# Whose engine makes the low halves of the key matrices: GpSimd instead of VectorE in the slab stage, with five gathered rows per slab instead of three

## What is computed

```python
def peer_ffn(h, w_q, sub_keys, u_tab, v_tab):
    tok = h.reshape(b * L, d)
    q = (tok @ w_q).astype(jnp.float32).reshape(n, PEER_HEADS, 2, PEER_DKEY // 2)
    s1 = jnp.einsum('nhk,ek->nhe', q[:, :, 0], sk[0])
    s2 = jnp.einsum('nhk,ek->nhe', q[:, :, 1], sk[1])
    ...
    gate = jax.nn.softmax(top_s, axis=-1)
    def run_block(args):
        t, g, e = args
        act = jax.nn.gelu(jnp.einsum('nd,nhkd->nhk', t, u_tab[e]), approximate=False)
        return jnp.einsum('nhk,nhkd->nd', g * act, v_tab[e])
```

## Time and profile before

| | us |
|---|---|
| runs of the kernel before (3) | 2326.02, 2326.99, 2332.55 |
| median | 2326.99 |
| profiled execution, its own time | 2322.12 |
| span of the profile in it | 2320.3 |
| slab stage (from the trace) | 1356 to 1608 |
| tail | 1608 to 1660 |
| value stage | 1665 to 2286 |

### The profile page before, as it was taken

The page is one execution under the profiler, slowest core; times in us unless marked ns, Lnnn a source line. Parts: engine busy times, 40 slices in busy tenths (PEclk is TensorE's granted clock), DMA queues, the critical chain, the costliest instruction groups (busy, mean ns, idle before and its releaser), DMA issues.

```text
span 2320.3 us, 34474 instructions
## 1 busy us (share of the span) xinstructions
PE 2108.4 (91%) x12253; PEld 1755.1 (76%) x12253; DVE 1546.9 (67%) x3300; ACT 745.0 (32%) x1111; POOL 814.7 (35%) x498
## 2 busy tenths in 40 slices
PE   7988899998979997999999989999898899898983
PEld 7988895555643347999999989999777777677772
DVE  1155314555572331179779889998888889898898
ACT  2122113443430002134434346654323232333231
POOL 2322330000210003346776641112644355565550
PEclk9998999999988998999999999999999999999997
DMA  9999996875968674235666667788999999999992
GB/s 356 356 357 345 345 356 272 337 310 195 311 243 302 232 282 133 65 108 170 216 222 222 211 229 285 278 300 344 388 394 394 393 393 393 385 394 377 394 393 89
DMA packets 200422, 682.89 MB, mean 294 GB/s; under 512 B 18432, under 2 KB 84352, under 8 KB 194304
## 3 DMA queue, kind: packets, MB, share of 16 engines
q1 hardware_dynamic: 151696, 508.36, 61.1%
q0 software_dynamic: 46080, 167.79, 19.1%
q10 hardware_dynamic: 2544, 5.48, 0.6%
HBM read 618.78 MB, written 196.32 MB: 351 GB/s over the span
## 4 chain that ended last, share of the span: by engine, by line
PE 33%; issue 23%; DMA 22%; DVE 15%; POOL 4%; ACT 3%; SPq 0%; ACTq 0%; DVEq 0%; POOLq 0%
DMA overlay<-peer_v 16%; PE bank L188 7%; PE bank L189 7%; PE bank L190 7%; DMA overlay<-peer_u 3%; DVE overlay L2142 3%; DVE arena L1964 2%; POOL overlay L1535 2%; PE bank L1951 2%; DVE arena L1959 2%; POOL overlay L340 2%; PE bank L601 2%; PE bank L585 2%; PE bank L651 1%; PE bank L624 1%
## 5 line engine op out<-in xcount | busy, mean ns | idle before, releaser
L188 PE MATMUL bank<-overlay 128*128 128x384 f32 (+4 forms) x2856 | 983.6, 344 | 110.6 <-DVE overlay L2146 64.4
L189 PE MATMUL bank<-overlay 128*128 128x384 f32 (+4 forms) x2856 | 967.2, 339 | 0.0
L190 PE MATMUL bank<-overlay 128*128 128x384 f32 (+4 forms) x2856 | 966.1, 338 | 0.0
L188 PEld LDWEIGHTS bank<-overlay 128*128 128x128 f32 x2856 | 556.3, 195 | 164.5 <-issue 85.6
L189 PEld LDWEIGHTS bank<-overlay 128*128 128x128 f32 x2856 | 556.2, 195 | 30.6
L190 PEld LDWEIGHTS bank<-overlay 128*128 128x128 f32 x2856 | 554.9, 194 | 32.3
L1535 POOL TENSOR_TENSOR overlay<-overlay 128x1024 fp32r<-128x1024 f32 x98 | 253.7, 2594 | 196.5 <-ACT overlay L1527 196.3
L1794 POOL DMA_INDIRECT arena<-peer_v,arena x160 | 239.7, 1498 | 180.7 <-DVE arena L1964 165.1
L1794 POOL DMA_INDIRECT arena<-peer_rows,arena x136 | 161.4, 1187 | 327.4 <-DVE arena L1959 307.0
L1964 DVE SCALAR_TENSOR_TENSOR arena<-arena 128x1024 f32<-128x1024 f32 x160 | 204.5, 1278 | 0.1
L1527 ACT CAST overlay<-overlay 128x1024 fp32r<-128x1024 f32 x144 | 150.8, 1049 | 142.1 <-DMA overlay<-peer_u 137.3
(11 more groups left out here) (233 smaller groups left out, 2073.9 us busy)
## 6 DMA issues: line engine op xcount, KB each, us to landing
overlay<-peer_u SPq DMA_DIRECT2D x128, 512.0 KB
overlay<-peer_v SPq DMA_DIRECT2D x128, 512.0 KB
o_ks<-cache_k SPq DMA_DIRECT2D x16, 4088.0 KB, 27.1
o_vsall<-cache_vall SPq DMA_DIRECT2D x16, 4088.0 KB, 37.5
arena<-cache_kT SPq DMA_DIRECT2D x32, 896.0 KB, 11.7
arena<-cache_v SPq DMA_DIRECT2D x56, 512.0 KB, 6.5
arena<-w_out SPq DMA_DIRECT2D x48, 512.0 KB, 5.8
act<-arena SPq DMA_DIRECT2D x128, 192.0 KB
```

The lines of the kernel that those rows point to most:

```text
L188: pe.matmul(out, lhs[0], rhs[0], start=start, stop=False)
L189: pe.matmul(out, lhs[0], rhs[1], start=False, stop=False)
L190: return pe.matmul(out, lhs[1], rhs[0], start=False, stop=stop)
```

## The change

- `ROW_TURNS` goes from (2, 5, 7) to (1, 2, 4, 5, 7): VectorE does five `dot`s per slab, 60 in the slab stage for 36. `DONE` goes from 60 to 84 with the tail's 24, and the rows left for the value stage from 236 to 212.
- VectorE's 46 low parts of rows 82 to 127 are gone (36 of them in the slabs, 10 in the tail); GpSimd makes them in `pool_gather`, between its gathers, with the same function as for the earlier rows. The count `u_lo2` is gone: TensorE and SyncE wait for `u_lo` throughout.
- The two gelus of row sums stand after three and after six groups of value matrices.

```diff
+        query_lo = []
...
+            query_lo.append(lo)
...
-        ROW_TURNS = (2, 5, 7)
+        ROW_TURNS = (1, 2, 4, 5, 7)
         SLAB_ROWS, TAIL_ROWS = SLABS * len(ROW_TURNS), (PK - TAIL) * 2
+        DONE_ROWS = SLAB_ROWS + TAIL_ROWS
...
-            for g in range(2 * UROWS - EARLY_ROWS):
+            def low(a):
+                if EARLY + LEAD <= a < PK:
+                    query_lo[0](QF + a, a % 4)
+
+            for g in range(RING):
+                gather(g)
+            g = RING
+            for a in range(EARLY, PK):
+                low(a + LEAD)
+                for k in range(2):
+                    if g < DONE_ROWS and (a >= TAIL or k * UPS + (a - EARLY) % UPS < len(ROW_TURNS)):
+                        gather(g)
+                        g += 1
+            for g in range(g, 2 * UROWS - EARLY_ROWS):
                 gather(g)
...
-                    fetch(a + 4, a % 4, (u_lo, QF + a + 1) if a < EARLY + LEAD else (u_lo2, a - (EARLY + LEAD) + 1))
+                    fetch(a + 4, a % 4, (u_lo, QF + a + 1))
...
-                    pe.wait_ge(*((u_lo, QF + a + 1) if a < EARLY + LEAD else (u_lo2, a - (EARLY + LEAD) + 1)))
+                    pe.wait_ge(*((u_lo, QF + a + 1)))
...
-            def low(a):
-                if EARLY + LEAD <= a < PK:
-                    dve.wait_ge(u_hi, QF + a + 1)
-                    dve.tensor_tensor(us[1][:, a % 4], uraw[a % 4], us[0][:, a % 4].bitcast(F32), ALU.subtract).then_inc(u_lo2, 1)
...
-                    if k in (0, 3, 6):
-                        low(EARLY + n * UPS + k // 3 + LEAD)
...
-                low(a + LEAD)
...
-            with act.Fori(0, 5) as x:
+            with act.Fori(0, 3) as x:
...
-            with act.Fori(5, 7) as x:
+            with act.Fori(3, 6) as x:
...
-            with act.Fori(7, PAIRS) as x:
+            with act.Fori(6, PAIRS) as x:
```

More of the change, by code:

```diff
@@ L1769, in layer @@
         u_done, gelu_done = sem("u_done"), sem("gelu_done")
-        u_lo2 = sem("u_lo2")
         hot_ready, g_done, g_kept = (sem(n) for n in ("hot_ready", "g_done", "g_kept"))
```

## The result

The changed kernel takes 2397.28 us (median of four runs, 2393.41 to 2398.23); the kernel before, in runs beside it, 2327.76 (2326.02 to 2332.55, four runs). The ratio is 1.029, interval 1.0272 to 1.0309: **69.5 us slower**. The sign was forecast, and that GpSimd's low parts would hold VectorE; the time was not: 2366 was forecast, and the range ended at 2390.

A forecast was written before the change was run, and what follows sets the result against it. VectorE and TensorE were taken to bound the slabs at about 20 us, DMA the value stage. Slabs +64, tail +7, value stage -32 gave +39: 2361 us profiled, 2366 on the median; forecast's own range 2354 to 2390, wider 2338 to 2390.

The forecast's parts named there:

- The bound: Slab stage: VectorE and TensorE both bound a slab at about 20 us before; after, VectorE at 25.3, TensorE waiting.
- the price of a low part: Slab stage: each GpSimd low part holds VectorE 2.2 us (1.91 at least, 2.40 at most), 79.2 us for 36.
- The slab stage: All slab terms, -40.7 + 27.4 + 1.6 + 79.2 = +67.5, less 3.1 of VectorE waiting for TensorE: +64 us.
- the other small terms: Slab stage, VectorE: 36 low parts go, -40.7 us; 24 dots come, +27.4; first dot waits for its landing, +1.6.
- Tail: After the slabs: GpSimd's turn of 4.9 to 6.4 us exceeds TensorE's 4.2 per row; +7 us, between 5.7 and 14.7.
- Value stage: 24 gathered rows fewer, 12.6 MB at 0.393 MB/us: -32 us; -29 if VectorE's dots were the true bound.
- A: Slabs: VectorE and GpSimd run side by side, low parts hide, slab stays at 19.8 to 20; -27, 2299 us; chance 0.09.
- the point from which it decides: Rival A, slabs: +39 falls to nothing if a low part holds VectorE for 1.1 us, to -7 at 0.9.
- B: Slabs: one-hot TENSOR_SCALARs are not held, a low part costs 1.5 us; 25 less, 2341 us; chance 0.11.
- C: Slabs: TensorE's clock falls in pauses; at the lower level half the time, slab about 30 us, 2420; chance 0.05.
- D: Slabs: GpSimd's low parts come late and TensorE waits; at 1 us per key row, 36 more, 2402 us; chance 0.03.

The follow-up runs named there:

- low_before_gather: The changed kernel, but GpSimd waits for the next dot before a low part and makes it before the gather: 2372.92 us, ratio 1.0158.
- low_apart: The changed kernel, with GpSimd's low part moved some 0.3 us away from the gather ahead of it, in the first four slabs alone: 2389.53 us, ratio 1.0249.
- apart_all: The changed kernel, with the low part moved away from the gather ahead of it in all twelve slabs: 2359.99 us, ratio 1.0157.
- lows_alone: The changed kernel with three dots per slab as before, GpSimd still making the low parts, gelus at their old places: 2397.18 us, ratio 1.0282.
- rows_alone: The kernel before, with five dots per slab and VectorE still making the low parts: 2330.19 us, ratio 0.9996.
- tail_lows: As rows_alone, but GpSimd makes the ten low parts of the tail: 2331.2 us, ratio 1.0025 against the kernel before.

## Why the prediction was wrong, point by point

**The bound.** Right. VectorE bounds the slabs, TensorE waits for it, GpSimd doesn't.

**The step that failed: the price of a low part.** The forecast had 36 x 2.2 = 79.2 us, "2.69 - 0.29 = 2.40 at most, 1.91 at least". Measured were 36 x 2.69 = 96.8, 17.6 more, and the upper end of the range was too low as well. The wrong step is "each of the 36 low parts costs VectorE its own length less start and end that overlap": a VectorE instruction can be held for more than one low part's length, because it can begin in the last part of the GpSimd instruction ahead and is then held through both. In `pool_gather` nearly each low part follows a gather at once. A TENSOR_SCALAR that begins in the last 0.3 to 0.7 us of the gather doesn't end there; it ends 0.09 us behind the low part: 0.67 + 2.41 + 0.09 less the 0.335 that it takes anyway is 2.84, and 0.31 + 2.40 + 0.09 - 0.335 = 2.47 behind the shorter gather of each slab. A low part that stands apart meets a TENSOR_SCALAR that begins 0.44 us inside it, and costs 2.07 or 2.08: the value that the forecast took, within 0.13. low_before_gather, low_apart and apart_all show this three times, and low_apart shows both prices inside one execution. That the gather alone is not enough is shown too: beside gathers with no low part behind them no TENSOR_SCALAR of the changed kernel takes over 0.43 us. Why the two together hold it was not shown.

The trace of before had such rows. 0.6 us behind the TENSOR_SCALAR of 1182.54, from which the lower bound was read, stands an instruction that takes 0.29 us the four other times (VectorE, then GpSimd):

```profile
1185.36 3.04 DVE L1699 SCALAR_TENSOR_TENSOR arena<-arena 128x128 f32<-128x128 f32 x1
```

```profile
1184.86 0.95 POOL L1545 DMA_INDIRECT arena<-peer_rows,arena  x1
1185.83 2.41 POOL L1535 TENSOR_TENSOR overlay<-overlay 128x1024 fp32r<-128x1024 f32 x1
```

It began 0.45 us before the end of a gather, with a low part 0.02 us behind it, and ended 0.16 behind the low part: 2.75 us lost. And the upper bound's own row, 1208.61, is of this kind too: its instruction began 0.24 us before the end of the first low part of a pair and was let through only behind the second. So 2.40 was no "at most"; with 2.75 the upper end of this term would have been 99, over the 96.8 measured.

**The slab stage.** Forecast +64, measured +83.5. The holds are 17.6 of the 19.5 missing. Most of the rest is the 0.28 us per slab in which VectorE still waits for TensorE, 3.4 in all for twelve slabs (3.0 in the window above), which the forecast had taken off; the other small terms come out 1.5 lower.

**Tail.** Forecast +7 between 5.7 and 14.7, measured +9.5. TensorE waits there for GpSimd's low parts, as forecast (waits, window 1698 to 1762):

```profile
PE bank L188 <- POOL overlay L1537: 8.6, 6, 2.2
```

and GpSimd in the tail:

```profile
1724.25 2.36 POOL L1537 TENSOR_TENSOR overlay<-overlay 128x1024 fp32r<-128x1024 f32 x1
1726.77 1.76 POOL L1797 DMA_INDIRECT arena<-peer_rows,arena  x1 [0.16 <-issue]
...
1729.80 2.38 POOL L1537 TENSOR_TENSOR overlay<-overlay 128x1024 fp32r<-128x1024 f32 x1
```

A turn is 1729.80 - 1724.25 = 5.6 us, between the 4.9 and the 6.4 of the forecast and over TensorE's 4.2. The other runs go the same way: tails of 59.8 to 63.6 us with whole low parts on GpSimd (lows_alone, low_before_gather, low_apart, apart_all), 54.2 to 56.5 with half, short ones or memsets, 51.9 and 52.8 with VectorE's; rows_alone and tail_lows, with the long gathers, are outside this order (66.3 and 66.7).

**Value stage.** Forecast -32 with -29 as the other end, measured -28.6, and between 26.1 and 29.8 in the eight other runs with five dots, against the one profile of before. The other end lies nearer, but the second profile with the old number of rows, lows_alone, took 608.7, so that a difference of 3 us between bytes (32) and VectorE (29) is not decided. Bytes went on at the full rate: DMA share 1.04 at 391 GB/s in 1700 to 2240 before, 1.04 at 389 in 1800 to 2330 after, and 0.5% of 578 is 3 us by itself. Against this profile of before, 3.4 us of the total go by it.

**Sum.** 39 + 19.5 (slabs) + 2.5 (tail) + 3.4 (value stage) + 1.4 + 6.1 (ahead of the slabs, by chance) - 0.6 = 71.3.

**The rivals.** A (side by side) is out; but the point from which it decides was near: the forecast said 1.1 us per low part. The runs give the time against the price per low part: 2.69 costs 69.5 us, 2.07 and 2.08 cost 42 and 32, 1.70 costs 14; 1.16 gains 6, 0.40 gains 13 (each against before on its own chip, the tail's ten low parts in it). No change lies between 1.16 and 1.70. B (TENSOR_SCALARs not held) is out: 35 of the 36 low parts fell on one. C (the clock falls in the pauses) is out in its price, though the clock did fall. TensorE in a slab:

```profile
1490.66 0.34 PE L190 MATMUL bank<-overlay 128*128 128x384 f32 x1
1493.27 1.69 PE L1967 MATMUL bank<-arena 128*128 128x128 f32 x8 [2.27 <-DVE arena L1996]
...
1495.08 0.52 PE L189 MATMUL bank<-overlay 128*128 128x384 f32 x1
```

Behind the pause of 2.27 us the matmuls take 0.52 for 0.34, the lower of the two levels, for 3.4 us once in each slab, and the clock of the stage is 0.92 for 0.99. TensorE's slack of some 7 us per slab hides it, as forecast. (C's own price was off: 12 x 5 more on 2366 is 2426, not 2420.) D is out: no wait for a low part in the slabs.

## What to carry to other kernels

Work that is moved from VectorE to GpSimd isn't off VectorE when both run on SBUF: here 1.13 us of VectorE's own subtraction became 2.1 to 2.8 us of standing still. Price such a move by the GpSimd instruction's length, and look at what runs on GpSimd directly ahead of it: behind a gather 0.3 us of distance was worth 0.6 us per instruction. And before writing "at most", go through all rows of the kind, with their neighbours: the trace of before held a hold of 2.75 us, half a microsecond behind the row from which a bound was read.

## What the runs showed of the hardware that was not expected

- A GpSimd instruction 0.02 us behind a gather holds a VectorE TENSOR_SCALAR that began up to 0.67 us earlier, inside the gather: 2.84 us lost for a low part of 2.41, where 0.30 us of distance leaves 2.08. A SCALAR_TENSOR_TENSOR of 128x128 and a first one-hot were held in the same way (3.04 us for 0.29, 3.46 for 0.68), and one instruction from the end of one low part through the next (2.69 for 0.29).
- A memset of GpSimd (128x1024, 0.97 us) holds a TENSOR_SCALAR as a subtraction does, for 1.16 us, but not a dot with two operands from SBUF (1.23 us beside it), which a subtraction in the tail holds for 2.0 us (3.22 for 1.22) and, behind a gather, up to 2.8 (4.00).
- A low part of 0.5 us straight behind a gather cost 0.40 us, less than its length: the TENSOR_SCALAR that began in the gather ended with the gather (0.68 us for 0.335), and only the one that began in the low part was held to its end (0.48). One of 1.29 us already holds the first kind through, for 1.71.
- With VectorE without a gap a single gather can take 8.6 or 23.5 us where its neighbours take 1.2 to 1.5. Each was seen once, in the two profiles with five dots and VectorE's own low parts; in the first three others took 3.99, 3.98 and 5.23. The cause is open.
